# High weight parts 128 bytes apart, low-rank attention heads in pairs, gate tiles ahead of the scores in B and C

## The reference

```
c_q, c_kv, k_r, hq, hf, hi, hgate, mq, gates = split(u @ w_in)
# mla: q = (rmsnorm(c_q) @ w_uq).reshape(.., 8 heads, 96)    96 = 64 without + 32 with a rotary turn
#      k_nope = (rmsnorm(c_kv) @ w_uk).reshape(.., 8, 64); v likewise; k_rope = rope(k_r), shared by the heads
#      softmax((q_nope . k_nope + rope(q_rope) . k_rope) * 96**-0.5, causal) @ v
# hg : a gated recurrence of 4 heads, in pairs of levels;  mem: attention over 256 memory tokens
x += (sum_b sigmoid(gates_b) * (y_b @ w_o_b)) @ w_out
```

## Time and profile before

| | |
|---|---|
| median of 3 runs | 2771.82 us (2770.63 to 2774.06) |
| the profiled execution, its span | 2774.93 us, 2773.0 us |
| TensorE busy | 2710.4 us of the span, 98% |
| VectorE, ScalarE busy | 1842.0 us (66%), 1300.2 us (47%) |
| chain of waits, by engine | PE 85%, DVE 8%, ACT 4% |

### The profile page before, as it was taken

How to read it: one execution, slowest core, us unless ns; L and a number is a source line. 1 busy time by engine, 2 the same in 40 slices (tenths; PEclk the granted TensorE clock), 3 DMA queues, 4 the chain that set the end, 5 groups by cost and what they waited for, 6 DMA issues and landing times.

```text
span 2773.0 us, 51136 instructions
## 1 busy us (share of the span) xinstructions
PE 2710.4 (98%) x21992; PEld 2578.3 (93%) x21992; DVE 1842.0 (66%) x3008; ACT 1300.2 (47%) x1860; POOL 72.8 (3%) x70
## 2 busy tenths in 40 slices
PE   8999999999999999999999999999999999999998
PEld 8999799999999879999999988899999998888997
DVE  6678566666666766767666547766666653776665
ACT  5445444444444545455444334544464433454443
POOL 0000010000000010000000001100000000110000
PEclk9999999999999999999999999999999999999999
DMA  7554356555555445555565653456555565345553
GB/s 265 190 168 134 114 172 202 183 194 196 189 186 163 127 152 164 184 187 187 196 204 170 195 154 122 107 171 198 183 183 191 179 194 155 124 106 171 190 195 103
DMA packets 481280, 474.50 MB, mean 171 GB/s; under 512 B 47104, under 2 KB 464416, under 8 KB 480928
## 3 DMA queue, kind: packets, MB, share of 16 engines
q1 hardware_dynamic: 477472, 460.75, 52.2%
q0 software_dynamic: 3584, 10.49, 1.4%
HBM read 464.91 MB, written 6.29 MB: 170 GB/s over the span
## 4 chain that ended last, share of the span: by engine, by line
PE 85%; DVE 8%; ACT 4%; issue 2%; DMA 1%; DVEq 0%; SPq 0%; ACTq 0%
PE ps L967 31%; PE ps L1066 31%; PE ps L1087 16%; PE ps L1128 2%; DVE WL L1908 2%; ACT WH L1527 2%; PE ps L1173 1%; PE ps L1209 1%; DVE REGION L2063 1%; PE ps L1014 1%; PE ps L1018 1%; DVE MX L2070 1%; DVE REGION L2096 1%; PE ps L1010 1%; DMA RAW<-in_w_in 0%
## 5 line engine op out<-in xcount | busy, mean ns | idle before, releaser
L1908 DVE TENSOR_TENSOR WL<-RAW,WH 128x2048 fp32r<-128x2048 f32 (+2 forms) x390 | 871.9, 2241 | 456.3 <-ACT WH L1527 454.4
L1527 ACT ACTIVATE WH<-RAW 128x2048 fp32r<-128x2048 f32 (+2 forms) x398 | 737.2, 1866 | 140.6 <-DMA RAW<-in_w_in 73.7
L1087 PE MATMUL ps<-HH,WH 128*128 128x256 f32 x1408 | 388.6, 276 | 0.0
L1087 PE MATMUL ps<-HH,WL 128*128 128x256 f32 x1408 | 388.6, 276 | 0.0
L1087 PE MATMUL ps<-HL,WH 128*128 128x256 f32 x1408 | 388.6, 276 | 0.0
L967 PE MATMUL ps<-UH,WH 128*128 128x256 f32 x1328 | 377.3, 284 | 5.0 <-DVE WL L1908 5.0
L967 PE MATMUL ps<-UL,WH 128*128 128x256 f32 x1328 | 369.1, 278 | 0.0
L967 PE MATMUL ps<-UH,WL 128*128 128x256 f32 x1328 | 368.9, 278 | 0.0
L1066 PE MATMUL ps<-UH,WH 128*128 128x256 f32 x2688 | 363.3, 277 | 1.2 <-DVE WL L1908 1.1
L1066 PE MATMUL ps<-UH,WL 128*128 128x256 f32 x2688 | 360.3, 276 | 0.0
L1066 PE MATMUL ps<-UL,WH 128*128 128x256 f32 x2688 | 360.2, 276 | 0.0
(11 more groups left out here) (330 smaller groups left out, 3661.7 us busy)
## 6 DMA issues: line engine op xcount, KB each, us to landing
RAW<-in_w_ffn_in SPq DMA_DIRECT2D x88, 1024.0 KB, 5.1
RAW<-in_ffn_wi SPq DMA_DIRECT2D x88, 1024.0 KB, 5.0
RAW<-in_w_in SPq DMA_DIRECT2D x86, 1024.0 KB, 5.2
RAW<-in_w_ffn_out SPq DMA_DIRECT2D x32, 1024.0 KB, 4.9
RAW<-in_ffn_wo SPq DMA_DIRECT2D x32, 1024.0 KB, 4.9
RAW<-in_w_out SPq DMA_DIRECT2D x16, 1024.0 KB, 4.9
RAW<-in_w_ffn_out SPq DMA_DIRECT2D x16, 768.0 KB, 4.2
RAW<-in_ffn_wo SPq DMA_DIRECT2D x16, 768.0 KB, 4.2
```

The source lines that it names most:

```text
L1087: last = nc.tensor.matmul(bank(n + side, 0, T), a[:, k, side * P:(side + 1) * P], b[:, k0 + k, :], start=k0 + k == 0 and a is wh and b is ...
L1527: nc.scalar.activation(split_ap(s, part_high(s)), raw_ap(s), ACT.Copy).then_inc(weights_high, 1)
L1908: v_.tensor_tensor(split_ap(s, part_low(s)), raw_ap(s), split_ap(s, part_high(s)).bitcast(FP), ALU.subtract)\
```

## The change

**Addresses.** A gap of 32 words (128 bytes) stands between each raw/low part and its high part; the overlays move so that everything stays on multiples of 128. By the allocation, low and high parts then start, modulo 512, at 0 and 128, 128 and 256, 256 and 384 in places 0 to 2, at 256 and 384, 384 and 0, 0 and 128, 0 and 128, 128 and 256 in places 3 to 7. The activations' parts stay where they were.

**Pairs of heads.** The host lays out `w_uq` so that each half has the 64 plain columns of four heads and then their four times 32 rotary ones. `uq` makes 6 products of 128 rows (two heads' plain rows; the third the rotary rows of four heads, evicted whole into `QR`), `uk` 4 of 128 rows; ScalarE evicts a pair with two copies of 64 rows. `swap` makes 2 products of four matmuls, each on its own 32 rows and 32 columns of TensorE and all in one bank, and one for the key. VectorE turns four heads at once. The cosine and sine tables fill all 128 partitions.

**Order in B and C.** The gate tiles stand ahead of the later scores in each step, in the numbering and on TensorE. The lists of VectorE and ScalarE keep their order.

```diff
-OVERLAYS = {3: 11376, 4: 15472, 5: 19568, 6: 16, 7: 4112}
+OVERLAYS = {3: 11344, 4: 15472, 5: 19600, 6: 16, 7: 4144}
+GATES_FIRST = ("B", "C")
...
+        unit = gated_unit(kind, step)
+        gates = gate_tiles(kind, unit) if unit is not None else []
+        if kind in GATES_FIRST:
+            for m in gates:
+                f[m] = n
+                n += 1
         if step + 3 < units:
             s[step + 3] = n
             n += n_s
...
-        pl.slabs(L + "uq", [4, 4], places=MIX)
+        pl.slabs(L + "uq", [3, 3], places=MIX)
-        pl.slabs(L + "uk", [8], places=MIX)
+        pl.slabs(L + "uk", [4], places=MIX)
-        pl.products(L + "swap", 5)
+        pl.products(L + "swap", 3)
...
             low.append(nc.alloc_sbuf_tensor_at(f"WL{i}", [P, SLOT], FR, offset=at))
+            sb(f"APART{i}", [P, APART])
             high.append(sb(f"WH{i}", [P, SLOT], FR))
...
+                    if kind in GATES_FIRST:
+                        issue_gates()
+                        issue_scores()
+                    else:
+                        issue_scores()
+                        issue_gates()
...
-                    for m in range(4):
-                        n = first[L + "uq"] + 4 * i + m
-                        product(n, [(bank(n)[0:QK, 0:T], [(slot(s, 3, 384)[:, k, m * QK:(m + 1) * QK], CQ[:, k, :]) for k in range(3)])])
+                    for m in range(3):
+                        n = first[L + "uq"] + 3 * i + m
+                        product(n, [(bank(n, 0, T), [(slot(s, 3, 384)[:, k, m * P:(m + 1) * P], CQ[:, k, :]) for k in range(3)])])
...
-                for m in range(4):
-                    n = first[L + "swap"] + m
-                    product(n, [(bank(n)[64:96, :], [(swap, QH[64:96, 2 * m:2 * m + 2, :])])])
+                for i in range(2):
+                    n = first[L + "swap"] + i
+                    product(n, [(bank(n)[r:r + ROPE, 0:T], [(con("swap", ROPE, slice(r, r + ROPE)), QR[r:r + ROPE, i, :])])
+                                for r in range(0, P, ROPE)])
...
+            def evict_heads(n, dst, h):
+
+                wait_product(act, n)
+                nc.scalar.activation(dst[0:NOPE, h, :], bank(n)[0:NOPE, 0:T], ACT.Copy)
+                nc.scalar.activation(dst[0:NOPE, h + 1, :], bank(n)[NOPE:2 * NOPE, 0:T], ACT.Copy).then_inc(evicted[n % BANKS], 1)
...
+                    v_.tensor_tensor(TMP[:, i, 0:T], bank(n, 0, T), SIN[:], ALU.mult).then_inc(evicted[n % BANKS], 1)
+                    link(v_.tensor_tensor(QR[:, i, :], QR[:, i, :], COS[:], ALU.mult))
                     wait_evicted(dve, n)
-                    link(v_.tensor_tensor(q, q, cos2, ALU.mult))
-                    link(v_.tensor_tensor(q, q, turned, ALU.add))
+                    for j in range(4):
+                        r = slice(j * ROPE, (j + 1) * ROPE)
+                        last = v_.tensor_tensor(QH[64:96, 4 * i + j, :], QR[r, i, :], TMP[r, i, 0:T], ALU.add)
```

More of the change, by code:

```diff
@@ L122, in constants @@
     swap = np.zeros((P, ROPE), np.float32)
-    for i in range(ROPE // 2):
-        swap[64 + ROPE // 2 + i, i] = -1.0
-        swap[64 + i, ROPE // 2 + i] = 1.0
+    for r in range(0, P, ROPE):
+        for i in range(ROPE // 2):
+            swap[r + ROPE // 2 + i, i] = -1.0
+            swap[r + i, ROPE // 2 + i] = 1.0
     put("swap", swap)
@@ L337, in attention_numbers @@
             n += n_s
[L338 to L341, removed]
+        if kind not in GATES_FIRST:
+            for m in gates:
+                f[m] = n
+                n += 1
         if step >= 0:
@@ L552, in build @@
         MK, MV = region(4, T), region(NT, 512)
-        used[0] = both - 2 * 2 * 2 * 260
+        used[0] = both - 2 * 2 * 2 * 260 - 2 * T
+        QR = region(2, T)
         Z, HK = region(HG_H * T), region(HG_H * T)
@@ L1174, in attention @@
                             last.then_inc(product_done, 1)
[L1175 to L1196, removed]
+                    def issue_scores():
+                        if step + 3 < units:
+                            for b, groups in enumerate(scores(step + 3)):
+                                if n_s == n_b:
+                                    n = s[step + 3] + b
+                                    product(n, [(bank(n)[:, g * T:g * T + k.shape[-1]], [(q, k)]) for g, (q, k) in enumerate(groups)])
+                                else:
+                                    for g, (q, k) in enumerate(groups):
+                                        n = s[step + 3] + 2 * b + g
+                                        product(n, [(bank(n, 0, k.shape[-1]), [(q, k)])])
@@ new lines, in issue_gates @@
+                    def issue_gates():
+                        unit = gated_unit(kind, step)
+                        if unit is not None:
+                            for m in gate_tiles(kind, unit):
+                                sl = slab_first[name] + (m - EARLY if kind == "C" else m) // 2
+                                cols = slice(m % 2 * P, (m % 2 + 1) * P)
+                                if m // 2 >= GATES_SPLIT.get(kind, DK):
+                                    wait_split(pe, sl)
+                                    terms = feature(parts(sl, DK, 256), UP, DK, cols)
+                                else:
+                                    wait_weights(pe, sl)
+                                    terms = [(slot(sl, DK, 256)[:, k, cols], U[:, k, :]) for k in range(DK)]
+                                product(f[m], [(bank(f[m], 0, T), terms)])
@@ L1277, in _ @@
                 wait_weights(pe, s)
-                for m in range(MLA_H):
+                for m in range(MLA_H // 2):
                     n = first[L + "uk"] + m
-                    product(n, [(bank(n)[0:NOPE, 0:T], [(slot(s, 2, 512)[:, k, m * NOPE:(m + 1) * NOPE], CKV[:, k, :]) for k in range(2)])])
+                    product(n, [(bank(n, 0, T), [(slot(s, 2, 512)[:, k, m * P:(m + 1) * P], CKV[:, k, :]) for k in range(2)])])
                 s = slab_first[L + "uv"]
@@ L1284, in _ @@
                     tokens(first[L + "uv"] + m, [(bank(first[L + "uv"] + m), lambda k: slot(s, 2, 512)[:, k, :], m)], CKV, 2)
-                swap = con("swap", ROPE, slice(64, 96))
-                for h in range(MLA_H):
-                    wait_evicted(pe, first[L + "uq"] + h)
-                for m in range(4):
-                    n = first[L + "swap"] + m
-                    product(n, [(bank(n)[64:96, :], [(swap, QH[64:96, 2 * m:2 * m + 2, :])])])
-                n = first[L + "swap"] + 4
-                product(n, [(bank(n)[64:96, 0:T], [(swap, KR[64:96, 0, :])])])
+                for m in range(6):
+                    wait_evicted(pe, first[L + "uq"] + m)
+                for i in range(2):
+                    n = first[L + "swap"] + i
+                    product(n, [(bank(n)[r:r + ROPE, 0:T], [(con("swap", ROPE, slice(r, r + ROPE)), QR[r:r + ROPE, i, :])])
+                                for r in range(0, P, ROPE)])
+                n = first[L + "swap"] + 2
+                product(n, [(bank(n)[64:96, 0:T], [(con("swap", ROPE, slice(64, 96)), KR[64:96, 0, :])])])
                 pe.wait_ge(pairs_summed, l + 1)
@@ L1728, in _ @@
                     evict(first["bias"], ROWS[0:BIAS_H, :], bank(first["bias"])[0:BIAS_H, :])
[L1729 to L1732, removed]
+                for i in range(2):
+                    for m in range(2):
+                        evict_heads(first[L + "uq"] + 3 * i + m, QH, 4 * i + 2 * m)
+                    n = first[L + "uq"] + 3 * i + 2
+                    evict(n, QR[:, i, :], bank(n, 0, T))
+                for m in range(MLA_H // 2):
+                    evict_heads(first[L + "uk"] + m, KH, 2 * m)
                 gate0, gate1 = slab_first[L + "hg.gate0"], slab_first[L + "hg.gate1"]
@@ L2381, in _ @@
                 feed.to(slab_first[L + "hg.gate0"])
[L2383 to L2388, removed]
+                for i in range(2):
+                    if i == 1:
+                        for m in range(2):
+                            wait_evicted(dve, first[L + "hg.o"] + m)
                         v_.tensor_tensor(HG_SQ, OT, OT, ALU.mult).then_inc(squares_ready, 1)
                         feed.to(slab_first[L + "hg.gate0"] + 1)
-                    n = first[L + "swap"] + m
-                    q = QH[64:96, 2 * m:2 * m + 2, :]
-                    turned = TMP[64:96, m % 2, :].rearrange("p (g t) -> p g t", g=2)
+                    n = first[L + "swap"] + i
                     wait_product(dve, n)
-                    v_.tensor_tensor(turned, bank(n)[64:96, :].rearrange("p (g t) -> p g t", g=2), sin2, ALU.mult)\
-                      .then_inc(evicted[n % BANKS], 1)
+                    v_.tensor_tensor(TMP[:, i, 0:T], bank(n, 0, T), SIN[:], ALU.mult).then_inc(evicted[n % BANKS], 1)
+                    link(v_.tensor_tensor(QR[:, i, :], QR[:, i, :], COS[:], ALU.mult))
                     wait_evicted(dve, n)
```

(11 more changed lines are left out.)

20 lines of the change are left out of this document (10 added, 10 removed).

## The result

The changed kernel takes 2799.85 us (median; 2797.81 to 2801.69) where the kernel before takes 2772.94 (2770.63 to 2775.30): a ratio of 1.0097, 95% interval 1.0079 to 1.0114, so 27 us slower. 2758 was predicted, with a range up to 2773.

A forecast was written before the change was run, and what follows sets the result against it. It took TensorE's own instructions, busy 98% of the span, and its few waits to bound the kernel. Terms -12.2 - 5.0 - 2.3 - 2.7 - 9 + 13.8 + 3.3 = -14.1 us gave 2758 us, range 2739 to 2773.

The forecast's parts named there:

- Gates first in B: In B, gate tiles ahead of scores add waits on banks; VectorE loses 8.6 us, 7.5 net; B 6.1 and 7 us longer.
- uq and uk, two layers: Pairs of heads need fewer TensorE instructions in both products: 2.6 and 3.5 us saved a layer, 12.2 us in all.
- swap: Sixteen instructions of 256 columns, four side by side, replace eight of 512: 2.5 us saved a layer, 5.0 for two.
- wait before gate1: TensorE's 1.14 us wait for the low part of gate1's first slab goes in both layers: 2.3 us saved (0 to 2.3).
- clock in hg.o: First layer's hg.o, granted half clock after the swap, runs at full clock after a short one: 2.7 us saved.
- addresses: Split matmuls: a +128 step from low to high part ends slow stretches, saving 9 us of a possible 11.0.
- B: Both layers' B with gates in front, half clocks included: 13.8 us longer together (0 to 17).
- C: In C, gate 0 before scores 1 delays the first transposes; later steps neutral: 1.6 us a layer, 3.3 lost (0 to 5).
- The first: In B and C the order costs nothing, gates filling TensorE's waits: -31.2 us, 2740.6; chance 0.25.
- The second: Split matmuls keep the slow pace, set by something other than the stationary start: -5.1 us, 2766.7; chance 0.17.
- the fourth: Swap runs serially and the clock falls in it again: +5.0 + 2.7 us, 2766; chance 0.10.
- The third: Split matmuls with stationary starts at 128 and 256 are slow for good: 2801 us; chance 0.10.

## Why the prediction was wrong

**The step that failed** is "Gates first in B", in the sentence that VectorE's "list from there to the end of B is nearly without pause: it loses 8.6 us". I followed the banks of gates 0 and 1, which ScalarE frees, up to the first values, and took the rest of B as VectorE's unchanged list. I didn't go on to the tiles that VectorE itself frees, although the same numbering (one gate tile, eight before the next transposes) is in each step. It holds 7.8 us of waits a layer, shown by the run that moved that line alone. By term:

| term | predicted | measured |
|---|---|---|
| uq and uk, two layers | -12.2 | -12.3 |
| swap | -5.0 | -5.1 |
| wait before gate1 | -2.3 | -2.7 |
| clock in hg.o | -2.7 | -2.9 |
| addresses | -9 | -0.6 (-3.1 to +1.9) |
| B | +13.8 | +34.9; alone 34.4 |
| C | +3.3 | +9.1; alone 9.4 |

(The first four rows are stage differences in the changed trace: 2.57 + 3.59 a layer, 2.57 a layer, 1.40 and 1.34, 6.35 - 3.45.) The measured column adds up to 20; the remaining 6.5 us are in the main half clocks at other places, 3.6 us just ahead of the second B. Such windows stand ahead of one B or both in three of the four runs with the pairs and scores first (not in the one with 64 bytes), and ahead of the first B in the run with the addresses alone. With the pairs alone they stand at 199.1, 1680.5, 2363.2 and 2383.6 us, 3.4 us each, and fit the pairs being worth 20.5 and not 23.0. What decides where one falls was not tried, and the prediction had no term for it.

**B in parts.** The start was right in mechanism and nearly in size: 7.3 us of waits for ScalarE, first values at 26.1 us instead of 24.3; 1.5 of the difference is gate 2 at half clock. The missed waits are 15.7 of the 21 us by which B was under-priced. The clock is the rest and a little more: I took 0.7 us for both layers, and TensorE's busy time grew by 2.8 and 5.3 (the slow pace of some gate tiles is in it).

**C.** Right in kind, a third of the size. Its first transposes wait 2.20 us for the probabilities where they waited 0.33, so 1.9 more, within the 1.4 to 1.9 I gave. I then wrote that later steps neither gain nor lose. They lose: two more waits of 0.67 us a layer, and in the first 0.5 for L2151. The first C's waits are 5.1 us in all, 2.3 before, which is 2.8 of its 4.1. The rest is a half clock from 1788.2 to 1791.6, which I had not priced; with the gates first in C alone each C has one of 3.4 us too, so it is C's own.

```profile
PE ps L1183 <- DVE REGION L2127: 3.5, 3, 2.2
PE ps L977 <- DVE REGION L2142: 0.7, 1, 0.7
PE ps L1231 <- DVE REGION L2151: 0.5, 1, 0.5
PE ps L1231 <- ACT REGION L1518: 0.4, 1, 0.4
```

**Addresses.** That a step of +128 turns slow into fast rested on 6 changes of slab of 8, all at a passage from one slab to another. In the alternating order, where each third matmul makes the step, slow stretches last as before and take 119 ns instead of 117.8. Part of the gain in the feed-forwards is paid there. What begins a slow stretch, and why the pace keeps, stays open.

**The rivals.** The first (the order costs nothing) is refuted most clearly. The second (no gain from the addresses) is what their run alone shows, and the fourth is out: the swap took 0.90 us at full clock. The third gave 2801 us, next to the measured 2799.85, and had nothing to do with it: 128 and 256 are not slow for good, since addresses alone cost nothing. A mechanism of that kind does exist, at odd multiples of 64 bytes. A time that fits is no evidence for its cause.

The Trainium skill has two rules that these runs speak to. TensorEngine Tiling (Array Packing), section "Restrictions and Gotchas", says that different row tiles can't use one PSUM bank at the same time; the swap's two products, each with four row tiles in one bank, have sixteen instructions of 256 columns and took 0.90 us together, so here they did. SBUF — State Buffer, section "A bandwidth-pool intuition that's wrong (but worth ruling out)", gives weight loads a port of their own; where only the stationary operand's start moved by 64 bytes, eight matmuls took 0.96 us instead of 0.90, so its address does count, whichever port serves it.

## What to carry to other kernels

An order that is changed on one engine, with PSUM banks handed out by number, moves every bank's next user; write out for each product who must have emptied bank n - 8 and where that stands in its engine's list, for a step in the middle and not only for the first. Move the lists of all engines together, and price even that: here 17 us stayed. Before a rule on addresses is built from transitions in a trace, run the address change alone: it took one kernel, and the result was nothing.

## What was not expected of the hardware

- Four 32x32 tiles on different rows and columns ran side by side into one PSUM bank: sixteen instructions, two such products, in 0.90 us, where eight of 512 columns one after another took 3.48.
- A split matmul's pace depends on the stationary operand's start: at multiples of 128 bytes 113.3 ns or, in a slow stretch, 117.8; at odd multiples of 64 about 119. A step of 64 bytes between the parts instead of 128 cost 51 us over the kernel.
- Between parts 128 bytes apart, a slow stretch of the alternating order has one matmul of 124 ns in six.
- In a pause of 5.9 us on TensorE, to 1710.58, the granted clock fell to 0.50 and stayed there until 1716.5, so that gate 2, begun at 1713.39, took 5.1 us for 3.6.
